# Query projections ahead of all convolutions in the selection block, with tap matrices built into the space of the normalised input

## The chip, the core and the metric

The kernel runs on one core of a Trainium2 chip. A core has a matrix engine (TensorE, PE in the profile), a vector engine (VectorE, DVE), a scalar engine (ScalarE, ACT), a general engine (GpSimd, POOL) and a queue that issues DMA transfers (SyncE, SP). Each runs its own list of instructions in order; they meet only at semaphores. The metric is the device time of one execution in microseconds (us).

## The reference

One layer of a decoder, over 1024 prompt positions and 8 x 8 sample positions (T = 1088 rows of D = 1024):

```python
h = rmsnorm(x, g_pre)
q, k, v, qi, ki, wi, ua, ub = split(h @ w_in)       # partial rotary on q, k, qi, ki
u = ua * sigmoid(ub)
score = sum_h wi_h * relu(qi_h . ki)                # keep the top 256 visible keys of each query
attn = softmax(q . k_selected) @ v_selected         # 8 heads, 2 key/value heads
c = causal depthwise conv(u, width 31) + b_dw; c = layernorm(c); c = c * sigmoid(c)
x = x + rmsnorm(concat(attn, c) @ w_out)
x = x + rmsnorm(relu(rmsnorm(x) @ w_up)^2 @ w_down)
```

## The kernel before

The kernel has four blocks, each closed by a barrier of all engines: projection and index scores, selection (`phase_select`), attention (`phase_attend`), output projection and MLP. The change lies in the selection block. Three things run in it side by side.

**The selection** (VectorE and ScalarE). A bit loop of 31 steps finds, for seven sets of rows, the bits of the 256th largest score: in each step VectorE counts over four sets (L1089), ScalarE over three (L945), and VectorE decides the bit from both. So a step ends when the later of the two is done. Two more counts follow, and then a tie loop over the seven sets: compare, running sum, select, add to the mask (L1164 to L1176). It needs the masks that ScalarE has scaled (`scale_masks`, L968).

**The convolution.** TensorE projects the 12 units of `u` (`uunits`, L1014) from the normalised input `hT`, ScalarE takes each unit from PSUM behind a step of the bit loop (`take_u`, L929 and L930; `behind` and `SIDE_PACE` say behind which), POOL multiplies (L838). After 12 units the rows go through DRAM into `up`, where each of the 32 groups (16 channels by 8 phases) holds one partition per channel and phase. A convolution of a group is then five matmul steps with a tap matrix of 128 x 640 values (`convolve`, L1051; the trace shows ten matmuls of 168 columns, two passes a step). POOL builds the tap matrix of a group by spreading the taps over a diagonal (`diagonal`, L853) into one of three slots in `stage`; group g waits until group g - 3 has been convolved. Three groups share a PSUM bank, ScalarE copies the bank back into `up` (`take_conv`, L936 and L938), and SP sends it to DRAM in two halves (L816): the first after 6 banks, the second after all 11.

**The queries.** `project_q` (L1040) computes 128 rows of q from `hT` into a bank, `take_q` (L919) copies them to one of three slots `zq`, POOL applies the rotary part (`rotate`, six small instructions, L868 to L875), TensorE turns them (`turn_q`, L1002), `take_turn` (L910) writes `qT`.

The order of TensorE is the list `EVENTS`: q0, c0, q1, c1, ..., q8, c8, c9, c10 (qi is a projection of a row block, ck a bank of convolutions), each over a bank of its own, six in turn. `turn_after` says after which event a query block is turned (two events later), and POOL follows the same list: rotate(i), then the three tap matrices of bank i. Since the tap matrices of a bank are queued behind the rotation of the same number, they wait for that projection and its copy.

At the end ScalarE copies the keys' high parts (`kH`, L983) and VectorE makes the low parts (L1182); then comes the barrier.

Of the kernel before, what the change touches and what calls it, by code (L numbers as in the profile page):

```python
# [26 lines left out]
P = 128  # L27
D = 1024
KC = D // P
# [3 lines left out]
T = SEQ + NB * NT  # L33
RT = SEQ // P + 1
# [53 lines left out]
MK_COLS = P * (SEQ // P) * (SEQ // P + 1) // 2  # L88

ACT_SETS = (2, 5, 6)  # L90
SIDE_PACE = 2.2

PH = 8
CG = P // PH
NCG = CC * PH
# [4 lines left out]
XRUN = XT - XS + 1  # L100
XO = T // PH
STEPS = 5
CONV_BANK = 3
# [530 lines left out]
def phase_select(nc, st, sem, sb_in, ps, bank, m, a, out):  # L634
# [15 lines left out]
    stage = sb_in(st, "stage", [P, 3 * STEPS * P])  # L650
    gate = stage[:, 0:768].rearrange("p (b t) -> p b t", b=2)
    ua = stage[:, 768:1536].rearrange("p (b t) -> p b t", b=2)
    wdiag = stage[:].rearrange("p (b n) -> p b n", b=3)
    dwp = sb_in(st, "dwp", [P, NCG, STEPS * PH])
    eye = sb_in(st, "eye", [P, CG])
    ulast = sb_in(st, "ulast", [P, CC, HIST])
# [66 lines left out]
    s_un = sem("s_un")  # L723


    EVENTS = [x for i in range(RT) for x in (("q", i), ("c", i))] + [("c", k) for k in range(RT, -(-NCG // CONV_BANK))]
    turn_after = {}
    for e, (kind, i) in enumerate(EVENTS):
        if kind == "q":
            turn_after.setdefault(min(max(e + 2, 4), len(EVENTS) - 1), []).append(i)  # L730
    TIE_ORDER = [NSET - 1] + list(reversed(range(NSET - 1)))

    def tie_sources(j):
# [27 lines left out]
    q_behind = {int(len(uunits) * SIDE_PACE + 1.4 * (i + 1)) + 1: i for i in range(3)}  # L761

    HIST_BIT = 4
    NCB = -(-NCG // CONV_BANK)

    conv_groups = lambda k: range(CONV_BANK * k, min(CONV_BANK * (k + 1), NCG))
    HEV = 2
# [1 line left out]
    with nc.Block() as block:  # L769
# [54 lines left out]
        @block.gpsimd  # L824
        def _(pool):
            nc.gpsimd.memset(usm[:], 0.0).then_inc(s_zero, 1)
            nc.gpsimd.memset(upr[:, :, :, 0:(HIST + 2) // PH], 0.0).then_inc(s_zero, 1)
            nc.gpsimd.memset(dwp[:], 0.0).then_inc(s_zero, 1)

            nc.gpsimd.tensor_copy(m["repb"][:], m["rep"][:])  # L830
            pool.wait_ge(s_c, 16 * CONSTS)
            for q, (n, c) in enumerate(uunits):
                t0, w = TCH[n]
                pool.wait_ge(s_g, q + 1)
                wp = min(w, SEQ - t0)
                x0 = (HIST + 2 + t0) // PH
                o = upr[:, c, :, x0:x0 + wp // PH].rearrange("p s x -> p x s")
                last = nc.gpsimd.tensor_tensor(o, ua[:, q % 2, 0:wp].rearrange("p (x s) -> p x s", s=PH),  # L838
                                               gate[:, q % 2, 0:wp].rearrange("p (x s) -> p x s", s=PH), ALU.mult)
                if wp < w:  # L840
                    nc.gpsimd.tensor_tensor(ulast[:, c, :], ua[:, q % 2, wp - HIST:wp], gate[:, q % 2, wp - HIST:wp],
                                            ALU.mult)
                    last = nc.gpsimd.tensor_tensor(unew[:, c, :], ua[:, q % 2, wp:w], gate[:, q % 2, wp:w], ALU.mult)
                last.then_inc(s_um, 1)
                if wp < w:
                    pool.wait_ge(s_um, q + 1)
                    nc.gpsimd.tensor_copy(usm[:, c, :, :].rearrange("p s (b x) -> p b s x", x=XS)[:, :, :, XS - 1],
                                          unew[:, c, :].rearrange("p (b t) -> p b t", t=NT)).then_inc(s_un, 1)

            def diagonal(g):  # L850
                if g >= 3:
                    pool.wait_ge(s_cg, g - 2)
                nc.gpsimd.tensor_tensor(wdiag[:, g % 3, :].rearrange("p (y c) -> p y c", c=CG),  # L853
                                        eye[:].unsqueeze(1).broadcast_to([P, STEPS * PH, CG]),
                                        dwp[:, g, :].unsqueeze(2).broadcast_to([P, STEPS * PH, CG]),
                                        ALU.mult).then_inc(s_dg, 1)

            def rotate(i):
                n = rows_of(i)
                zz = z[0:n, i % 3, :].rearrange("p (h d) -> p h d", d=HD)  # L860
                x1, x2 = zz[:, :, 0:HALF], zz[:, :, HALF:ROT]
                cos = cs[0:n, 0, i, :].unsqueeze(1).broadcast_to([n, NH, HALF])
                sin = cs[0:n, 1, i, :].unsqueeze(1).broadcast_to([n, NH, HALF])
                t = [rt[0:n, i % 2, k, :].rearrange("p (h d) -> p h d", d=HALF) for k in range(4)]
                pool.wait_ge(s_ze, i + 1)
                if i >= 2:
                    pool.wait_ge(s_rot, i - 1)
                nc.gpsimd.tensor_tensor(t[0], x1, cos, ALU.mult).then_inc(s_ro, 1)  # L868
                nc.gpsimd.tensor_tensor(t[1], x2, sin, ALU.mult).then_inc(s_ro, 1)
                nc.gpsimd.tensor_tensor(t[2], x2, cos, ALU.mult).then_inc(s_ro, 1)  # L870
                nc.gpsimd.tensor_tensor(t[3], x1, sin, ALU.mult).then_inc(s_ro, 1)
                pool.wait_ge(s_ro, 5 * i + 4)
                nc.gpsimd.tensor_tensor(x1, t[0], t[1], ALU.subtract).then_inc(s_ro, 1)
                pool.wait_ge(s_ro, 5 * i + 5)
                nc.gpsimd.tensor_tensor(x2, t[2], t[3], ALU.add).then_inc(s_rot, 1)  # L875

            pool.wait_ge(s_eye, 1)
            pool.wait_ge(s_dw, 16 * CC * PH)
            for g in conv_groups(0):
                diagonal(g)  # L880
            for kind, i in EVENTS:
                if kind == "q":
                    rotate(i)
                elif i >= 1:
                    for g in conv_groups(i):
                        diagonal(g)
            pool.wait_ge(s_dg, NCG)
            pool.wait_ge(s_z, RT)
            for kv in range(NKV):
                nc.gpsimd.memset(kL[(1 - kv) * HD:(2 - kv) * HD, kv, :].bitcast(F32), 0.0)  # L890

        @block.scalar
        def _(act):
# [74 lines left out]
                    nc.scalar.activation(mk, mk, ACT.Copy, scale=BIG, bias=-BIG).then_inc(s_ms, 1)  # L968

            taken = [i for it, i in q_behind.items() if it < BITS]  # L970
            for e, (kind, i) in enumerate(EVENTS):
                if kind == "c":
                    take_conv(i)
                elif i not in taken:
                    take_q(i)
                for q in turn_after.get(e, ()):
                    take_turn(q)
                if e == 4:
                    scale_masks()
            act.wait_ge(s_z, RT)  # L980
            for kv in range(NKV):
                for half in (kv, 1 - kv):
                    nc.scalar.copy(kH[half * HD:(half + 1) * HD, kv, :], kT[kv * HD:(kv + 1) * HD, 0:SEQ]).then_inc(s_kh, 1)  # L983

        @block.tensor
        def _(pe):
# [57 lines left out]
            def convolve(e, k):  # L1044
                bank_free(e)
                for g in conv_groups(k):
# [1 line left out]
                    pe.wait_ge(s_dg, g + 1)  # L1048
                    o = bank[2 + e % 6][:, (g % CONV_BANK) * XRUN:(g % CONV_BANK + 1) * XRUN]
                    for j in range(STEPS):  # L1050
                        last = nc.tensor.matmul(o, wdiag[:, g % 3, j * P:(j + 1) * P], up[:, g, j:j + XRUN],  # L1051
                                                start=(j == 0), stop=(j == STEPS - 1))
                    last.then_inc(s_cg, 1)

# [1 line left out]
            for e, (kind, i) in enumerate(EVENTS):  # L1056
                if kind == "q":
                    project_q(e, i)
                else:
                    convolve(e, i)  # L1060
                if e == 3:
                    turn_new_rows()
                if e == 4:
                    pe.wait_ge(s_te, HEV + 2)
                for q in turn_after.get(e, ()):
                    turn_q(q)
# [1259 lines left out]
```

## Time and profile before

| | us |
|---|---|
| median of 3 runs | 1841.5 (1841.31 to 1841.74) |
| profiled execution | 1840.0 |
| span in its trace | 1838.2 |
| PE busy in the span | 1600.2 (87%) |
| DVE, ACT, POOL busy | 671.6, 618.4, 408.8 |
| first u projection of the selection block | 252.4 |
| last of 12 units taken by ScalarE | 402.3 |
| end of the tie loop on VectorE | 479.2 |
| last convolution copied, second half of the DMAs issued | 573.7 |
| first instruction of attention | 581.6 |

Busy time is an average over blocks with different limits; TensorE is nearly full in the MLP and far from it in the selection block. Times in the timelines count from the start of the span, and the bracket behind an instruction is the idle time of its engine before it and what ended that. PEclk is the granted clock of TensorE as a share of 2.4 GHz.

### The profile page before, as it was taken

How to read it: one execution, taken by the hardware profiler on the slowest of the kernel's cores; microseconds unless marked ns; L12 is line 12 of the kernel's file. 1: busy time of each engine (PE TensorE's matmuls, PEld its weight loads, DVE VectorE, ACT ScalarE, POOL GpSimd, SP SyncE). 2: the span in 40 equal slices, each digit the busy share in tenths (PEclk: the TensorE clock that was granted, in tenths of full speed). 3: DMA queues.
4: the chain of work that ended last, by engine and by line, in shares of the span. 5: the costliest groups of instructions: out<-in, count | busy, mean ns of one | idle time of the engine just before them, and what ended most of it. 6: DMA issues, size and time to landing. Idle time of an engine off the chain costs nothing.

```text
span 1838.2 us, 22486 instructions
## 1 busy us (share of the span) xinstructions
PE 1600.2 (87%) x8760; PEld 1357.4 (74%) x8760; DVE 671.6 (37%) x1310; ACT 618.4 (34%) x1100; POOL 408.8 (22%) x434
## 2 busy tenths in 40 slices
PE   4798889955776998985984999999999999999996
PEld 2366446534455875664984999999999999999995
DVE  1236547779402543244007222222222222222225
ACT  2215539883103776244227312121121212021212
POOL 2232001025335121001227112221221222122112
PEclk9999989987888999987996999999999999999997
DMA  5011041312023101314110011111111111111102
GB/s 200 6 45 55 1 117 54 62 32 35 1 49 111 78 2 69 115 46 155 46 46 0 29 41 46 43 38 46 46 34 46 46 41 39 46 46 35 46 24 109
DMA packets 100053, 97.67 MB, mean 53 GB/s; under 512 B 14822, under 2 KB 88630, under 8 KB 97668
## 3 DMA queue, kind: packets, MB, share of 16 engines
q1 hardware_dynamic: 96492, 75.71, 14.5%
q0 software_dynamic: 3488, 20.98, 3.1%
q8 instruction: 47, 0.77, 0.2%
q14 instruction: 26, 0.21, 0.0%
HBM read 85.55 MB, written 11.45 MB: 53 GB/s over the span
## 4 chain that ended last, share of the span: by engine, by line
PE 47%; DVE 2%; ACT 2%; POOL 1%; DMA 1%; issue 0%; POOLq 0%; DVEq 0%; ACTq 0%
PE ps L2073 16%; PE ps L2075 16%; PE ps L2074 16%; DMA out_y_p<-y 1%; DVE xlo L2165 1%; POOL stat L1962 0%; ACT hrow L2027 0%; POOL x L1976 0%; DVE xlo L2163 0%; ACT y L2017 0%; DVE y L2225 0%; DVE y L2229 0%; POOL stat L1958 0%; DMA gpost<-in_g_mlp_post 0%; DVE hlo L2197 0%
## 5 line engine op out<-in xcount | busy, mean ns | idle before, releaser
L1951 POOL TENSOR_TENSOR wlo<-wraw,whi 128x1024 fp32r<-128x1024 f32 x72 | 173.9, 2416 | 723.2 <-ACT whi L1995 723.2
L2073 PE MATMUL ps<-xhi,whi 128*128 128x384 f32 (+1 forms) x960 | 314.7, 328 | 18.6 <-DVE xlo L2165 18.6
L2075 PE MATMUL ps<-xhi,wlo 128*128 128x384 f32 (+1 forms) x960 | 314.3, 327 | 0.0
L2074 PE MATMUL ps<-xlo,whi 128*128 128x384 f32 (+1 forms) x960 | 314.1, 327 | 0.0
L2073 PE MATMUL ps<-hhi,whi 128*128 128x384 f32 (+1 forms) x768 | 257.3, 335 | 16.8 <-DVE hlo L2197 16.8
L2074 PE MATMUL ps<-hlo,whi 128*128 128x384 f32 (+1 forms) x768 | 256.3, 334 | 0.0
L2075 PE MATMUL ps<-hhi,wlo 128*128 128x384 f32 (+1 forms) x768 | 256.2, 334 | 0.0
L2073 PEld LDWEIGHTS ps<-xhi,whi 128*128 128x128 f32 x960 | 181.3, 189 | 19.2 <-issue 18.2
L1995 ACT CAST whi<-wraw 128x1024 fp32r<-128x1024 f32 x72 | 75.5, 1049 | 345.9 <-PE ps L2075 345.8
L2216 DVE TENSOR_TENSOR moT<-ps,moT 128x384 f32<-128x384 f32 x168 | 90.1, 536 | 259.5 <-PE ps L2075 259.5
L2074 PEld LDWEIGHTS ps<-xlo,whi 128*128 128x128 f32 x960 | 181.3, 189 | 0.0
L2075 PEld LDWEIGHTS ps<-xhi,wlo 128*128 128x128 f32 x960 | 181.2, 189 | 0.0
L2073 PEld LDWEIGHTS ps<-hhi,whi 128*128 128x128 f32 x768 | 147.3, 192 | 18.8 <-DVE hlo L2197 14.0
L2204 DVE TENSOR_TENSOR rel<-rel 128x384 f32<-128x384 f32 (+1 forms) x96 | 51.5, 536 | 296.0 <-ACT rel L2050 296.0
L2074 PEld LDWEIGHTS ps<-hlo,whi 128*128 128x128 f32 x768 | 147.2, 192 | 0.0
L2075 PEld LDWEIGHTS ps<-hhi,wlo 128*128 128x128 f32 x768 | 147.2, 192 | 0.0
L2050 ACT ACTIVATE rel<-ps 128x384 f32<-128x384 f32 (+1 forms) x96 | 45.5, 474 | 276.7 <-PE ps L2075 276.7
L1014 PE MATMUL ps<-hT,w 128*128 128x384 f32 (+1 forms) x384 | 122.0, 481 | 13.5 <-DMA w<-in_w_u 8.6
L1014 PEld LDWEIGHTS ps<-hT,w 128*128 128x128 f32 x384 | 74.6, 195 | 59.9 <-issue 10.2
L1051 PE MATMUL ps<-up,stage 128*128 128x168 f32 x320 | 63.6, 371 | 59.1 <-POOL stage L853 59.1
L1089 DVE TENSOR_SCALAR_CACHE_REDUCE mask<-moT,cand 128x384 bf16<-128x384 f32 (+3 forms) x132 | 109.0, 882 | 1.1
L1051 PEld LDWEIGHTS ps<-up,stage 128*128 128x128 f32 x320 | 61.3, 242 | 62.2 <-issue 62.2
(268 smaller groups left out, 2238.0 us busy)
## 6 DMA issues: line engine op xcount, KB each, us to landing
wraw<-in_w_up SPq DMA_DIRECT2D x32, 512.0 KB, 4.1
wraw<-in_w_down SPq DMA_DIRECT2D x32, 512.0 KB, 3.4
x<-in_x SPq DMA_DIRECT2D x16, 512.0 KB, 7.4
w<-in_w_rows SPq DMA_DIRECT2D x2, 2048.0 KB, 10.3
w<-in_w_u SPq DMA_DIRECT2D x2, 2048.0 KB, 10.8
wraw<-in_w_out SPq DMA_DIRECT2D x8, 512.0 KB, 4.2
out_y_p<-y SPq DMA_DIRECT2D x8, 512.0 KB, 2.6
up<-by_channel SPq DMA_DIRECT2D x32, 86.0 KB, 4.1
```

Source lines behind the costliest of these rows:

```text
L1014: last = nc.tensor.matmul(bank[2 + 2 * (q % 3) + half][:, 0:w], wslot[c // 2][:, k, col:col + P], hT[:, k, t0:t0 + w], start=(k == 0), sto ...
L1051: last = nc.tensor.matmul(o, wdiag[:, g % 3, j * P:(j + 1) * P], up[:, g, j:j + XRUN], start=(j == 0), stop=(j == STEPS - 1))
L1089: last = nc.vector.tensor_scalar(mk, sc, against[0:n, j:j + 1].bitcast(F32), None, op, ALU.add, accum_out=count[0:n, j:j + 1])
L1951: nc.gpsimd.tensor_tensor(wlo[:, par, :], wraw[:, par, :], whi[:, par, :], ALU.subtract).then_inc(s_wlo, 1)
L1995: nc.scalar.copy(whi[:, j % 2, :], wraw[:, j % 2, :]).then_inc(s_whi, 1)
L2050: nc.scalar.activation(rel[:, b % 3, 0:TCH[c][1]], bank[b % NBK][:, 0:TCH[c][1]], ACT.Relu).then_inc(s_re, 1)
L2073: nc.tensor.matmul(o, wh, xh, start=first, stop=False)
L2074: nc.tensor.matmul(o, wh, xl, start=False, stop=False)
L2075: return nc.tensor.matmul(o, wl, xh, start=False, stop=last)
L2165: nc.vector.tensor_tensor(in_time(xlo, t0, w), by_phase(t0, w), in_time(xhi, t0, w), ALU.subtract).then_inc(s_mlo, 1)
L2204: nc.vector.tensor_tensor(rel[:, b % 3, 0:w], rel[:, b % 3, 0:w], rel[:, b % 3, 0:w], ALU.mult).then_inc(s_sq, 1)
L2216: nc.vector.tensor_tensor(dst, src, dst, ALU.add).then_inc(s_ad, 1)
```

## The change

The projections of all nine query blocks now stand ahead of all eleven banks of convolutions on TensorE. The first three tap matrices stay in `stage`; the others go into 13 slots laid over `hT`, which nothing reads after the last projection, so `diagonal(3)` waits for all nine projections (`s_z`), and from group 16 on a slot waits for the group 13 before it. POOL's order is now: tap matrices 0 to 2, rotations 0 to 6, tap matrices 3 to 7, rotation 7, tap matrices 8 to 10, rotation 8, tap matrices 11 to 31. ScalarE turns and takes in an order of its own, copies the key parts after bank 2, and takes the other banks last. `SIDE_PACE` goes from 2.2 to 2.08, which moves the takes of u from steps 3, 5, 7, 9, 12, 14, 16, 18, 20, 23, 25, 27 of the bit loop to 3, 5, 7, 9, 11, 13, 15, 17, 19, 21, 23, 25, and the takes of q0 and q1 from steps 28 and 30 to 27 and 28, with q2 behind step 30.

```diff
-SIDE_PACE = 2.2
+SIDE_PACE = 2.08
...
-    wdiag = stage[:].rearrange("p (b n) -> p b n", b=3)
+    WN = STEPS * P
+    WS = 3
+    WH = KC * T // WN
+    flat = hT[:].rearrange("p k t -> p (k t)")
+    wdiag = [stage[:, g * WN:(g + 1) * WN] if g < WS else flat[:, (g - WS) % WH * WN:((g - WS) % WH + 1) * WN]
+             for g in range(NCG)]
...
-    EVENTS = [x for i in range(RT) for x in (("q", i), ("c", i))] + [("c", k) for k in range(RT, -(-NCG // CONV_BANK))]
-    turn_after = {}
-    for e, (kind, i) in enumerate(EVENTS):
-        if kind == "q":
-            turn_after.setdefault(min(max(e + 2, 4), len(EVENTS) - 1), []).append(i)
+    NCB = -(-NCG // CONV_BANK)
+    EVENTS = [("q", i) for i in range(RT)] + [("c", k) for k in range(NCB)]
+    turn_after = {6: (0, 1), 7: (2,), 8: (3, 4), 9: (5,), 10: (6,), 11: (7,), 12: (8,)}
...
             def diagonal(g):
-                if g >= 3:
-                    pool.wait_ge(s_cg, g - 2)
-                nc.gpsimd.tensor_tensor(wdiag[:, g % 3, :].rearrange("p (y c) -> p y c", c=CG),
+                if g == WS:
+                    pool.wait_ge(s_z, RT)
+                if g >= WS + WH:
+                    pool.wait_ge(s_cg, g - WH + 1)
+                nc.gpsimd.tensor_tensor(wdiag[g].rearrange("p (y c) -> p y c", c=CG),
...
-            for g in conv_groups(0):
+            for g in range(WS):
                 diagonal(g)
-            for kind, i in EVENTS:
-                if kind == "q":
-                    rotate(i)
-                elif i >= 1:
-                    for g in conv_groups(i):
-                        diagonal(g)
+            for i in range(RT - 2):
+                rotate(i)
+            for g in range(WS, WS + 5):
+                diagonal(g)
+            rotate(RT - 2)
+            for g in range(WS + 5, WS + 8):
+                diagonal(g)
+            rotate(RT - 1)
+            for g in range(WS + 8, NCG):
+                diagonal(g)
...
-            for e, (kind, i) in enumerate(EVENTS):
-                if kind == "c":
-                    take_conv(i)
-                elif i not in taken:
-                    take_q(i)
-                for q in turn_after.get(e, ()):
-                    take_turn(q)
-                if e == 4:
+            for i in range(RT - 3):
+                if i == 0:
+                    for q in range(len(taken), 3):
+                        take_q(q)
+                take_turn(i)
+                take_q(i + 3)
+                if i == 1:
                     scale_masks()
-            act.wait_ge(s_z, RT)
+            for i in range(RT - 3, RT):
+                take_turn(i)
+                take_conv(i - RT + 3)
             for kv in range(NKV):
                 for half in (kv, 1 - kv):
                     nc.scalar.copy(kH[half * HD:(half + 1) * HD, kv, :], kT[kv * HD:(kv + 1) * HD, 0:SEQ]).then_inc(s_kh, 1)
+            for k in range(3, NCB):
+                take_conv(k)
...
-                if e == 3:
+                if e == 1:
                     turn_new_rows()
-                if e == 4:
+                if e == 6:
                     pe.wait_ge(s_te, HEV + 2)
```

On TensorE, from the last projection of u on (`w,hT` is a query projection, `up,stage` or `up,hT` a bank of convolutions, `identf,zq` a turn of query blocks, four instructions each, `ulast` and `unew` the turn of the new convolution rows), before:

```order
L1040 MATMUL ps<-w,hT 128x512 x8
L1051 MATMUL ps<-up,stage 128x168 x15
L1040 MATMUL ps<-w,hT 128x512 x8
L1051 MATMUL ps<-up,stage 128x168 x15
L1023 MATMUL ps<-identf,ulast 30x128 x4
L1026 MATMUL ps<-identf,unew 64x128 x4
L1040 MATMUL ps<-w,hT 128x512 x8
L1002 MATMUL ps<-identf,zq 128x128 x8
L1051 MATMUL ps<-up,stage 128x168 x15
```

and now:

```order
L1051 MATMUL ps<-w,hT 128x512 x16
L1034 MATMUL ps<-identf,ulast 30x128 x4
L1037 MATMUL ps<-identf,unew 64x128 x4
L1051 MATMUL ps<-w,hT 128x512 x40
L1013 MATMUL ps<-identf,zq 128x128 x8
L1051 MATMUL ps<-w,hT 128x512 x8
L1013 MATMUL ps<-identf,zq 128x128 x4
L1051 MATMUL ps<-w,hT 64x512 x8
L1013 MATMUL ps<-identf,zq 128x128 x8
L1062 MATMUL ps<-up,stage 128x168 x15
L1013 MATMUL ps<-identf,zq 128x128 x4
L1062 MATMUL ps<-up,hT 128x168 x15
```

All 9 x 8 projections come first, with the wait for ScalarE's copies of the new rows behind the seventh; the first bank stands behind the turn of query block 4.

On POOL, around the rotation of query block 7 (`zq` and `rtq` are the rotation, `eye,dwp` a tap matrix), before:

```order
L873 TENSOR_TENSOR zq<-rtq 128x8x8
L875 TENSOR_TENSOR zq<-rtq 128x8x8
L853 TENSOR_TENSOR stage<-eye,dwp 128x640 x3
L868 TENSOR_TENSOR rtq<-zq,csq 128x64
L869 TENSOR_TENSOR rtq<-zq,csq 128x64
L870 TENSOR_TENSOR rtq<-zq,csq 128x64
L871 TENSOR_TENSOR rtq<-zq,csq 128x64
L873 TENSOR_TENSOR zq<-rtq 128x8x8
L875 TENSOR_TENSOR zq<-rtq 128x8x8
L853 TENSOR_TENSOR stage<-eye,dwp 128x640 x3
```

and now:

```order
L877 TENSOR_TENSOR zq<-rtq 128x8x8
L879 TENSOR_TENSOR zq<-rtq 128x8x8
L857 TENSOR_TENSOR hT<-eye,dwp 128x640 x5
L872 TENSOR_TENSOR rtq<-zq,csq 128x64
L873 TENSOR_TENSOR rtq<-zq,csq 128x64
L874 TENSOR_TENSOR rtq<-zq,csq 128x64
L875 TENSOR_TENSOR rtq<-zq,csq 128x64
L877 TENSOR_TENSOR zq<-rtq 128x8x8
L879 TENSOR_TENSOR zq<-rtq 128x8x8
L857 TENSOR_TENSOR hT<-eye,dwp 128x640 x3
```

Before, three tap matrices stood between two rotations, in the slots of `stage`; now five and three, in slots over `hT`, and only six tap matrices still have a rotation right in front of them.

## Rows read from the trace of the kernel before

**Rows 1.** The page, chain that ended last: shares of the span by engine.
```profile
PE 47%; DVE 2%; ACT 2%; POOL 1%; DMA 1%; issue 0%; POOLq 0%; DVEq 0%; ACTq 0%
```

**Rows 2.** Busy time by engine in two stretches of 20 us (columns in the first line).
```profile
core 0: us, PE busy (x) PEld busy (x) DVE busy (x) ACT busy (x) POOL busy (x), PEclk, DMA share, GB/s
440.00:460.00 20.00, 7.12 (x32) 6.79 (x33) 19.76 (x11) 4.90 (x9) 17.00 (x9) 0.57 0.00 1
500.00:520.00 20.00, 16.42 (x59) 10.66 (x58) 0.00 (x0) 1.64 (x4) 5.47 (x9) 0.91 0.17 31
```

**Rows 3.** Waits, 400 to 600 us: engine, line, waited for: us in total, times, longest.
```profile
POOL rtq L868 <- ACT zq L919: 88.2, 8, 12.2
...
PE ps L1051 <- POOL stage L853: 59.1, 9, 15.4
```

**Rows 4.** Timeline, PE: start us, us, engine, line, operation, count, [idle before it].
```profile
383.49 7.11 PE L1040 MATMUL ps<-w,hT 128*128 128x512 f32 x16 [3.51 <-ACT stage L930]
...
507.93 6.19 PE L1051 MATMUL ps<-up,stage 128*128 128x168 f32 x30 [3.58 <-POOL stage L853]
513.96 7.03 PE L1040 MATMUL ps<-w,hT 128*128 128x512 f32 x16
520.83 0.60 PE L1002 MATMUL ps<-identf,zq 128*128 128x128 f32 x4
```

**Rows 5.** Timeline, POOL, where VectorE runs counts or nothing.
```profile
404.62 3.73 POOL L853 TENSOR_TENSOR stage<-eye,dwp 128x640 f32<-128x640 f32 x3
...
521.69 0.32 POOL L868 TENSOR_TENSOR rtq<-zq,csq 128x64 f32<-128x64 f32 x1 [11.45 <-ACT zq L919]
...
523.31 0.32 POOL L875 TENSOR_TENSOR zq<-rtq 128x64 f32<-128x64 f32 x1
...
565.55 1.27 POOL L853 TENSOR_TENSOR stage<-eye,dwp 128x640 f32<-128x640 f32 x1 [0.15 <-PE ps L1051]
...
568.40 1.27 POOL L853 TENSOR_TENSOR stage<-eye,dwp 128x640 f32<-128x640 f32 x1 [0.15 <-PE ps L1051]
```

**Rows 6.** Timeline, POOL, beside VectorE's tie loop.
```profile
437.58 4.39 POOL L868 TENSOR_TENSOR rtq<-zq,csq 128x64 f32<-128x64 f32 x1 [12.25 <-ACT zq L919]
...
451.47 5.69 POOL L853 TENSOR_TENSOR stage<-eye,dwp 128x640 f32<-128x640 f32 x3
466.99 1.50 POOL L868 TENSOR_TENSOR rtq<-zq,csq 128x64 f32<-128x64 f32 x1 [9.83 <-ACT zq L919]
...
472.09 4.62 POOL L853 TENSOR_TENSOR stage<-eye,dwp 128x640 f32<-128x640 f32 x3
```

**Rows 7.** Timeline, DVE, the tie loop: two early instructions and the last.
```profile
437.43 4.43 DVE L1168 TENSOR_TENSOR_SCAN w<-w 64x2056 f32<-64x2056 bf16 x1
441.89 2.51 DVE L1171 SCALAR_TENSOR_TENSOR w<-w,need 64x2056 bf16<-64x2056 f32 x1
...
478.61 0.56 DVE L1176 SCALAR_TENSOR_TENSOR mask<-w,mask 128x384 bf16<-128x384 bf16 x1
```

**Rows 8.** Timeline, ACT, at the end of the bit loop.
```profile
398.37 0.83 ACT L945 ACTIVATE mask<-moT,cand 128x640 bf16<-128x640 f32 x1 [0.91 <-DVE cand L1106]
...
402.32 0.42 ACT L929 ACTIVATE stage<-ps 128x320 f32<-128x320 f32 x1
...
407.27 0.56 ACT L919 COPY zq<-ps 128x512 f32<-128x512 f32 x1
```

**Rows 9.** Timeline, the DMA queue of SP (issues), both halves of the outgoing convolution.
```profile
514.75 7.49 SPq L816 DMA_DIRECT2D by_time<-up  x16
523.96 0.34 SPq L820 DMA_DIRECT2D moT<-by_time  x1
573.69 7.47 SPq L816 DMA_DIRECT2D by_time<-up  x16
```

**Rows 10.** Windows of 1 us in one bank of convolutions (columns as in rows 2).
```profile
493.00:494.00 1.00, 1.00 (x5) 1.00 (x5) 0.00 (x0) 0.00 (x0) 0.17 (x1) 0.50 0.00 0
495.00:496.00 1.00, 1.00 (x9) 1.00 (x8) 0.00 (x0) 0.00 (x0) 0.00 (x0) 1.00 0.00 0
```

More of the change, by code:

```diff
@@ L763, in phase_select @@
     HIST_BIT = 4
-    NCB = -(-NCG // CONV_BANK)
     conv_groups = lambda k: range(CONV_BANK * k, min(CONV_BANK * (k + 1), NCG))
@@ L1050, in convolve @@
                     for j in range(STEPS):
-                        last = nc.tensor.matmul(o, wdiag[:, g % 3, j * P:(j + 1) * P], up[:, g, j:j + XRUN],
+                        last = nc.tensor.matmul(o, wdiag[g][:, j * P:(j + 1) * P], up[:, g, j:j + XRUN],
                                                 start=(j == 0), stop=(j == STEPS - 1))
```

## The prediction

> **What bounds the kernel now.** I read the chain that ended last first. Its parts name TensorE for 47% of the span and hardly anything else [rows 1], all of it the late MLP, so it says nothing of the block that changes; but the MLP and attention follow behind barriers, so what the selection block gives is what the kernel gives. Next come busy times over short stretches of that block: from 500 to 520 us TensorE is busy for 16.4 of 20 us, VectorE for none, ScalarE for 1.6 and POOL for 5.5; from 440 to 460 us TensorE has 7.1 while VectorE is full and POOL at 17.0 [rows 2]. So the first part runs beside VectorE, and the second is a chain through TensorE with holes. The waits name them: TensorE waits 59.1 us in 9 waits for tap matrices, and POOL 88.2 us in 8 waits for copies of a projection [rows 3]. POOL has time, but it stands in the wrong place of its list. The timeline shows one round: bank of convolutions 6.2 us, projection 6.9, turn 0.6, idle 3.58 for POOL, 17.1 in all [rows 4]. In that idle time POOL does a rotation of 1.9 us (521.69 to 523.63) and the first tap matrix, 1.24 of 3.73 [rows 5]. The block ends when the last bank is copied: SP then issues 16 transfers in 7.47 us from 573.69 on [rows 9], and attention starts.
>
> **The bit loop.** A step takes 4.95 us (402.32 to 407.27), and ScalarE idles 0.91 us in a step without a take [rows 8]; a take of q costs 0.56, so one more of them there costs nothing as long as its projection is ready. By the step length, u9, u10 and u11 are taken at 402.3 - 6 x 4.95 = 372.6, 382.5 and 392.4 us, ten us earlier than now. q0 and q1 need u9's banks, and run from 373.5 to 387.5 (about 7 each). The turn of the new rows then waits until POOL has multiplied u11: 2.3 us behind its take (402.32 to 404.62, [rows 5, 8]), so at 394.7. Five more projections of 6.87 (the distance 513.96 to 520.83, [rows 4]), 1 us for the turn and some 2 at the low clock bring TensorE to 432; turns 0 and 1 to 433; q7, turn 2 and q8 to 447.5. q0, q1 and q2 are taken at 402, 407 and 417, so TensorE has 15 us or more in hand at each. The wait for ScalarE's copies of the new rows is over at 420 and costs nothing behind q6. Seven of nine projections are now hidden under the bit loop and the two counts behind it, where only two or three were. SIDE_PACE alone gives nothing; it opens the banks.
>
> **POOL beside the tie loop.** This is where the price of the change lies. Rotation 3 can start at 434, when the tie loop starts. Without VectorE six rotation instructions take 1.9 us [rows 5]; beside it the first instruction alone took 4.39, and the rotation with three tap matrices took from 437.58 to 457.16, 19.6 us for 5.7 us of work [rows 6]. The first instruction ends at 441.97, within 0.1 us of the end of the running sum at 441.86 [rows 7]: POOL is held until VectorE's instruction is done. Further on, where VectorE's instructions are short, the same work took 466.99 to 476.71, 9.7 us: a rate of 0.59. The two tap triples beside it give 3.73/5.69 = 0.66 and 3.73/4.62 = 0.81.
>
> Rotations 3 and 4 cost from 434 to about 453.5. Then I take the rate 0.6. Rotations 5 and 6 (3.8 us) go to 460; tap matrices 3 to 7 (6.2) to 470; rotation 7, tap matrices 8 to 10 and rotation 8 (7.5) to 483. Tap matrix 11 is there at 484. VectorE, now disturbed by more POOL work, ends its loop about 5 us later than 479.2, near the same time; nothing waits for it but the low key parts, 2.4 us and long before the end. Bounds for tap matrix 11: at rate 1 from 453.5 on, 473; at the first stretch's rate of 5.7/19.6 = 0.29 until 484 and 1 behind it, 493.
>
> The Trainium skill, SBUF — State Buffer, section "Who interferes with whom", says that a VectorE instruction with two inputs in SBUF and a POOL instruction that reads SBUF exclude each other for a whole instruction, in order of issue. The trace agrees for the running sum. By that rule alone each of eight tap matrices would wait for a VectorE instruction of about 1.4 us, 2.6 in place of my 2.1, and tap matrix 11 would come 4 us later, the kernel at 1787; my sum goes by the measured rates.
>
> **The convolutions.** At full clock TensorE convolves a group in 1.43 us: POOL's tap matrices from 565.55 to 568.40 wait for one group each, (568.40 - 565.55) / 2 apart [rows 5]. At half clock it is twice that, 2.8 us (5 matmuls in a window of 1 us at a granted clock of 0.50 against 9 at 1.00, both counts with cut ends, [rows 10]). A tap matrix costs POOL 1.24 us free of waiting, so once VectorE is out of the way POOL keeps ahead of TensorE, and TensorE is the bound. Bank 0 runs at 454 to 460 behind the turn of block 4. Groups 3 to 10 follow their tap matrices, about 2 us apart, slower than 1.43; turns 5 to 8 (0.6 each) lie in the gaps, except 8. From 484: 21 groups by 1.43 = 30.0, the turn 0.6, the last copy 0.6, and 0.8 for a start at the low clock: 516.
>
> **The tail.** SP's first half must be through before the second: bank 5 (groups 15 to 17) is taken at about 494, behind the key copies; issue 7.49 and landing end 9.2 later (514.75 to 523.96, [rows 9]), at 503, before 516. So the second half starts at once. Key copies and low parts, which lay behind the last bank, are hidden now as before: SP's 7.47 us covered them. The clearing of the key halves by POOL, 2 us, is over with the last tap matrix. Attention starts earlier by the whole difference.
>
> Sum: 573.7 - 516 = 57.7 us. Against the profiled execution, 1840.0 us (span 1838.2 and 1.8 around it): 1782.3. The median of the runs is 1.5 us above that execution, so I say 1783. As a check, what TensorE still has before it when the tie loop begins: before, six projections (41), 26 groups by 6.19/3 = 2.06 (54), turns (4) and by difference some 37 of waiting for POOL, to 573; now two projections (14), 32 groups (47), turns (5) and 18 of waiting, to 516. The gain is four projections done earlier, 19 us of waiting, and 7 us of clock, since the groups run in one piece.
>
> **The rivals.**
>
> 1. *POOL gets through earlier.* If tap matrix 11 comes at 473, TensorE is the bound from bank 1 on: 460 + 29 x 1.43 + 2.4 for turns + 0.6 = 504.5, a saving of 69 and 1772. For it: 0.81 in the second triple [rows 6]. Against it: rotations do far worse than tap matrices, and two of them stand in front.
> 2. *TensorE at the low clock, or POOL held longer.* Waiting for tap matrices 2 us apart, it might lose its clock, and the later groups go at 2.8 us. Rows show 0.50 at the start of a bank, after 3.6 us of idling, and 1.00 within 4 us of steady work [rows 4, 10]. If the clock is low for half of 29 groups, 14 x 1.4 = 20 us are added; or tap matrix 11 comes at 493, 9 us. 1792 to 1803; I give the clock and the longer hold 0.08 each. Against it: at 2.8 us a group TensorE is never idle with matrices 2 us apart, and steady work brought the clock back each time. [...]
> 3. *Slower than before.* The takes of q0, q1 and q2 now stand in the bit loop in ScalarE's fixed order, and VectorE waits for ScalarE in each step. A projection that is late by n us there stops the selection for n us, and all that follows. TensorE is 15 us ahead at q2, the closest, and the change has 57 us to lose, so it must be 72 us late there, as if every projection took twice its 6.87 us and the units of u did too. 1845 if so. Nothing in the trace points to it.
> 4. *It does not do what it says*: the projections stay behind something that ends with the bit loop, such as the wait for the new rows at 420. Then all nine end only at 420 + 9 x 6.87 = 482, tap matrix 3 cannot start before (it needs all nine), and 29 groups take to 482 + 41.5 + 3 = 527: 1794. Against it: only q7 and q8 lie behind that wait in the list.
>
> **How the numbers follow.** The forecast has 0.60 (1776 to 1790), rival 1 0.14, rival 2 0.16, rival 4 0.06, rival 3 0.03, and 0.01 for a result near the old time. The range 1768 to 1799 leaves out rival 3, the end of rival 2, and what is below rival 1. A measurement of this kernel tells 0.2%, 3.7 us, from no change; all cases but the last two lie far outside it: faster 0.96, same 0.01, slower 0.03.
>
> **What would show it.** In the profile after, six projections would start before 425, all nine be done by 450; the 9 waits of convolutions for tap matrices be gone but for bank 1 to 3 (some 15 to 25 us together); tap matrices 3 to 10 lie at 460 to 483 at 1.5 to 2.2 us each; the last 20 groups run without a gap at 1.43 us, clock 1.0; SP's second half begins at 516. The bit loop must still end at 418 to 419. I would be wrong if ScalarE idles in it before a take of q, if tap matrices 3 to 10 take more than 3 us each, or if attention or the MLP change their length.

## The result, and the profile after

The changed kernel takes 1782.3 us (median of 4 runs, 1781.0 to 1783.0) against 1841.6 (1841.3 to 1842.3) in the same comparison: 0.968 of the time, 95% interval 0.966 to 0.969. The forecast was 1783. The profiled execution took 1781.0 us with a span of 1779.2.

The beginning of the bit loop differs by up to 4.3 us between the traces (260.76 to 265.09 us), and what differs lies ahead of the block. So I measure the block from its first count by ScalarE to the second half of the outgoing convolution on SP. These two rows are the first counts, of before and of after:

```profile
262.80 0.83 ACT L945 ACTIVATE mask<-moT,cand 128x640 bf16<-128x640 f32 x1 [19.30 <-DVE cand L1106]
```
```profile
260.98 0.83 ACT L953 ACTIVATE mask<-moT,cand 128x640 bf16<-128x640 f32 x1 [19.20 <-DVE cand L1117]
```

And the timeline of SP's queue after, which answers to [rows 9]:

```profile
494.43 7.47 SPq L818 DMA_DIRECT2D by_time<-up  x16
...
514.27 7.44 SPq L818 DMA_DIRECT2D by_time<-up  x16
```

Before, 573.69 - 262.80 = 310.9 us; after, 514.27 - 260.98 = 253.3. The block is 57.6 us shorter (the sum said 57.7). The spans differ by 59.0; the rest is the start, which lies 1.8 us earlier in this trace, less 0.4 behind the block. I call this distance the block's length below; each length is read from one trace. In all traces here TensorE's first instruction of attention follows 10.0 to 10.1 us behind SP's second half (583.74 before, 524.29 after), so what shortens the block shortens the kernel.

TensorE's timeline after, against [rows 4]:

```profile
371.75 13.97 PE L1051 MATMUL ps<-w,hT 128*128 128x512 f32 x32 [0.22 <-ACT stage L938]
392.68 1.03 PE L1034 MATMUL ps<-identf,ulast 128*30 128x128 f32 x4 [6.95 <-POOL unew L845]
...
394.36 35.85 PE L1051 MATMUL ps<-w,hT 128*128 128x512 f32 x80
...
450.80 6.56 PE L1062 MATMUL ps<-up,stage 128*128 128x168 f32 x30
...
463.87 6.91 PE L1062 MATMUL ps<-up,hT 128*128 128x168 f32 x30 [6.08 <-POOL hT L857]
...
476.79 1.66 PE L1062 MATMUL ps<-up,hT 128*128 128x168 f32 x10 [2.72 <-POOL hT L857]
...
483.00 1.67 PE L1062 MATMUL ps<-up,hT 128*128 128x168 f32 x10 [1.25 <-POOL hT L857]
...
484.98 28.79 PE L1062 MATMUL ps<-up,hT 128*128 128x168 f32 x200
```

There are three stretches: projections q0 to q6 under the bit loop and the two counts behind it, with one hole of 7 us; then banks with four waits, one for a rotation (3.9 us) and three for tap matrices; and the last 20 groups without a gap, 28.79 / 20 = 1.44 us each. The waits from 380 to 530 us, where [rows 3] had 59.1 us in 9 waits of TensorE and 88.2 in 8 of POOL:

```profile
POOL rtq L872 <- ACT zq L927: 29.3, 4, 13.1
...
PE ps L1062 <- POOL hT L857: 10.1, 3, 6.1
...
PE ps L1034 <- POOL unew L845: 7.0, 1, 7.0
...
PE ps L1013 <- POOL zq L879: 3.9, 1, 3.9
```

Windows of the same stretch (columns as in [rows 2]):

```profile
440.00:460.00 20.00, 13.88 (x55) 9.58 (x53) 19.65 (x15) 3.21 (x6) 19.69 (x17) 0.83 0.00 0
...
464.00:468.00 4.00, 4.00 (x15) 4.00 (x16) 3.93 (x3) 0.00 (x0) 4.00 (x3) 0.50 0.00 0
468.00:472.00 4.00, 4.00 (x28) 4.00 (x27) 3.97 (x3) 0.75 (x2) 4.00 (x3) 0.91 0.00 0
...
484.00:512.00 28.00, 28.00 (x198) 27.75 (x197) 22.90 (x2) 8.59 (x21) 25.37 (x22) 1.00 0.34 81
```

From 440 to 460 us TensorE had 7.1 of 20 before and has 13.9 now; VectorE and POOL are both full there. POOL's timeline, against [rows 5] and [rows 6]:

```profile
435.59 4.53 POOL L879 TENSOR_TENSOR zq<-rtq 128x64 f32<-128x64 f32 x1
...
462.21 8.96 POOL L857 TENSOR_TENSOR hT<-eye,dwp 128x640 f32<-128x640 f32 x5
...
475.38 4.36 POOL L857 TENSOR_TENSOR hT<-eye,dwp 128x640 f32<-128x640 f32 x3
...
481.59 25.89 POOL L857 TENSOR_TENSOR hT<-eye,dwp 128x640 f32<-128x640 f32 x21
```

POOL builds its tap matrices in three runs behind a rotation, of 5, 3 and 21. A tap matrix costs 1.79 us (8.96 / 5) and 1.45 (4.36 / 3) beside the tie loop, 1.23 (25.89 / 21) behind it. VectorE's timeline, against [rows 7], has a row that nobody forecast:

```profile
435.57 4.43 DVE L1179 TENSOR_TENSOR_SCAN w<-w 64x2056 f32<-64x2056 bf16 x1
...
477.09 1.51 DVE L1187 SCALAR_TENSOR_TENSOR mask<-w,mask 128x384 bf16<-128x384 bf16 x1
486.88 22.91 DVE L1193 TENSOR_TENSOR keys<-kT,keys 64x1024 fp32r<-64x1024 f32 x2 [8.28 <-ACT keys L992]
```

The two low parts of the keys take 22.9 us together, from 486.88 to 509.79, while POOL builds its 21 tap matrices. They are done 4.5 us before SP's second half begins at 514.27, so nothing waits for them.

### The profile page after: what moved, and what is told of

It reads as the page before. It is cut to its first block, busy times and chain, and to the rows that moved or that the text cites. A ratio compares the mean times of both kernels' runs of the same rounds, so it can differ in the third digit from the quotient of the medians.

```text
span 1779.2 us, 22486 instructions
## 1 busy us (share of the span) xinstructions
PE 1584.5 (89%) x8760; PEld 1344.1 (76%) x8760; DVE 693.8 (39%) x1310; ACT 618.1 (35%) x1100; POOL 419.2 (24%) x434
## 4 chain that ended last, share of the span: by engine, by line
PE 49%; DVE 2%; ACT 2%; POOL 1%; DMA 1%; issue 0%; POOLq 0%; DVEq 0%; ACTq 0%
PE ps L2084 16%; PE ps L2086 16%; PE ps L2085 16%; DMA out_y_p<-y 1%; DVE xlo L2176 1%; POOL stat L1973 0%; ACT hrow L2038 0%; POOL x L1987 0%; DVE xlo L2174 0%; ACT y L2028 0%; DVE y L2236 0%; DVE y L2240 0%; POOL stat L1969 0%; DMA gpost<-in_g_mlp_post 0%; DVE hlo L2208 0%
## 5 line engine op out<-in xcount | busy, mean ns | idle before, releaser
L2084 PEld LDWEIGHTS ps<-xhi,whi 128*128 128x128 f32 x960 | 181.4, 189 | 19.1 <-issue 18.2
L465 PE MATMUL ps<-w,hT 128*128 128x328 f32 (+3 forms) x256 | 95.4, 527 | 0.0
L465 PEld LDWEIGHTS ps<-w,hT 128*128 128x128 f32 (+1 forms) x256 | 47.4, 190 | 39.3 <-issue 27.6
```

The lines of the kernel that those rows point to most:

```text
L465: last = nc.tensor.matmul(bank[2 + u % 2][0:n, 0:w], hT[:, k, i * P:i * P + n], wslot[g % 2][:, k, 0:w], start=(k == 0), stop=(k == KC - 1))
L2084: nc.tensor.matmul(o, wh, xh, start=first, stop=False)
```

## Where the gain comes from

The forecast gave the credit to the projections done early and called SIDE_PACE a mere opener. The first five experiments take the parts apart. Ratios are to the kernel before in the same comparison, with 95% intervals. That kernel's median was between 1837 and 1842 us, so across sections ratios are compared, or the block's lengths, and not times.

**SIDE_PACE alone, in the kernel before.**

```
-SIDE_PACE = 2.2
+SIDE_PACE = 2.08
```

> The kernel before with SIDE_PACE 2.08 alone. The prediction says that this alone gives nothing: 1841.6 us. Rival, from the row of the rotation beside the tie loop: with q1 and q2 taken ten us earlier, rotation 2 runs at about 426 us, ahead of the tie loop, and takes 2 us in place of 14; the fourth bank of convolutions starts at about 457 in place of 473.5, and some 12 us remain at the end: 1829.

1827.6 us, 0.993 (0.992 to 0.994): the rival's value. The block's length is 560.99 - 263.61 = 297.4, 13.5 less. The first bank of convolutions starts 9.9 us earlier, counted from the start of the block (396.94 - 263.61 against 406.04 - 262.80), and in POOL's timeline the third rotation is now through before the tie loop starts:

```profile
396.94 5.97 PE L1051 MATMUL ps<-up,stage 128*128 128x168 f32 x30 [15.44 <-POOL stage L853]
```
```profile
428.32 0.32 POOL L868 TENSOR_TENSOR rtq<-zq,csq 128x64 f32<-128x64 f32 x1 [12.21 <-ACT zq L919]
...
430.23 3.73 POOL L853 TENSOR_TENSOR stage<-eye,dwp 128x640 f32<-128x640 f32 x3
```

In [rows 6] the same rotation and three tap matrices took 19.6 us. The waits of this kernel from 400 to 600 us:

```profile
PE ps L1051 <- POOL stage L853: 37.3, 9, 11.7
```

[Rows 3] has 59.1 us in the same stretch, but with the first bank's wait of 15.4, which here ends before 400. Without it that is 43.7 against 37.3. So most of the 13.5 us is that the chain starts 9.9 us earlier and keeps that lead through the tie loop; the waits give the smaller part. The sentence "SIDE_PACE alone gives nothing" is wrong in the old order.

**POOL's list alone.** The kernel before, with the tap matrices of bank i put ahead of rotation i; the order on TensorE and ScalarE, the three buffers of `stage` and the pace of 2.2 stay. A tap matrix needs nothing of a projection.

```
-            for kind, i in EVENTS:
-                if kind == "q":
-                    rotate(i)
-                elif i >= 1:
+            for i in range(NCB):
+                if i >= 1:
...
+                if i < RT:
+                    rotate(i)
```

> The kernel before with POOL's list alone changed (tap matrices of a bank ahead of the rotation of the same number), SIDE_PACE left at 2.2. Theory (the tie loop holds POOL whatever came ten us earlier, so the two edits overlap): 1786, some 2 us above the same with 2.08. Rival (the two add up, 13 us for the pace by the run that changed it alone): 1797.

1782.3 us, 0.970 (0.969 to 0.972), the block's length 514.82 - 260.76 = 254.1 against the changed kernel's 253.3. One reordered list gives, within what can be told here, the whole gain, with the projections where they were. TensorE's waits for tap matrices from 400 to 600 us, against 59.1 in [rows 3]:

```profile
PE ps L1051 <- POOL stage L853: 17.0, 5, 15.4
```

The longest, 15.4, is that of the first bank, at the end of the bit loop. Behind it 1.6 us are left in four waits.

**The same list with the pace of 2.08.**

> The kernel before, order of TensorE and ScalarE as it was, SIDE_PACE 2.08, and only POOL's list changed: the tap matrices of a bank stand before the rotation of the same number, in the three slots of stage. Theory (order on POOL is the whole effect; all projections first is not needed): no 3.6 us of idling and no half clock in a round, 11.9 us a round in place of 17.1, the last bank at about 517: 1785. Rival (projections must be out of the way): the rounds keep most of their length, 1810 or more.

1783.6 us, 0.969 (0.968 to 0.970): the theory's value. TensorE's timeline shows a round, against [rows 4]:

```profile
481.74 4.44 PE L1051 MATMUL ps<-up,stage 128*128 128x168 f32 x30
486.02 7.03 PE L1040 MATMUL ps<-w,hT 128*128 128x512 f32 x16
492.88 0.60 PE L1002 MATMUL ps<-identf,zq 128*128 128x128 f32 x4
```

A round is 493.32 - 481.74 = 11.6 us where it was 17.1. Of the 5.5 us, 3.6 are the idle time and 1.75 the bank's start at the low clock (6.19 to 4.44); both go because the three tap matrices are built while TensorE projects. The interval overlaps that at 2.2: pace and list do not add. With 2.08 TensorE comes to the turn of a query block while POOL still does that rotation beside the tie loop; it waits 8.17 us there, which it does not at 2.2, and the bank behind it takes 6.80 us:

```profile
454.83 1.11 PE L1002 MATMUL ps<-identf,zq 128*128 128x128 f32 x4 [8.17 <-POOL zq L875]
```

So what the pace wins ahead of the tie loop is lost in it.

**No space in `hT`.** The changed kernel with all 32 tap matrices in the three buffers of `stage`.

```
-    wdiag = [stage[:, g * WN:(g + 1) * WN] if g < WS else flat[:, (g - WS) % WH * WN:((g - WS) % WH + 1) * WN]
+    wdiag = [stage[:, g % WS * WN:(g % WS + 1) * WN]
...
-                if g == WS:
-                    pool.wait_ge(s_z, RT)
-                if g >= WS + WH:
-                    pool.wait_ge(s_cg, g - WH + 1)
+                if g >= WS:
+                    pool.wait_ge(s_cg, g - WS + 1)
```

> The changed kernel with all tap matrices in the three slots of stage, group g waiting for the convolution of group g - 3; nothing is laid over the normalised input. Theory (order decides, and with three slots TensorE still sets the pace at 1.43 us a group): 1782 to 1784. Rival (the space is what lets POOL run ahead, and without it POOL and TensorE wait for each other): at least 0.3 us a group over 29 groups, 1791 or more. By the theory VectorE's low key parts also get in between two tap matrices again, 1.2 us each in place of 22.9 for both.

1783.8 us, 0.970 (0.968 to 0.971), length 253.1. The space in the normalised input is worth nothing that can be told here: POOL needs 1.24 us for a tap matrix and TensorE 1.43 for a group, so three buffers feed it. POOL and VectorE in that kernel:

```profile
490.21 1.27 POOL L855 TENSOR_TENSOR stage<-eye,dwp 128x640 f32<-128x640 f32 x1 [0.21 <-PE ps L1060]
```
```profile
490.34 4.45 DVE L1191 TENSOR_TENSOR keys<-kT,keys 64x1024 fp32r<-64x1024 f32 x2 [8.28 <-ACT keys L990]
```

Where POOL waits 0.15 to 0.2 us for each buffer, the low parts of the keys take 4.45 us, not 22.9.

**The old pace in the changed kernel.**

> The changed kernel with SIDE_PACE back at 2.2. Theory (POOL beside the tie loop sets the start of the convolutions): rotation 3 starts at 440 in place of 432, tap matrix 3 at about 468 in place of 462, so 1788 against 1782. Rival (the chain of projections on TensorE sets it): all ten us of delay come out at the end, 1792. Rival (POOL is held by the tie loop whatever its start): 1782.

1783.6 us, 0.970 (0.968 to 0.972), length 517.45 - 261.73 = 255.7, 2.4 more than with 2.08: near the rival by which the loop holds POOL whatever its start. POOL starts rotation 3 at 442.82 where it was 431.83, but does rotations 3 and 4 in 10.0 us (to 452.79) where it took 18.0 (to 449.80), and reaches tap matrix 3 only 3 us later than in the changed kernel:

```profile
465.21 8.96 POOL L857 TENSOR_TENSOR hT<-eye,dwp 128x640 f32<-128x640 f32 x5
```

What POOL does ahead of time meets the long instructions at the front of VectorE's loop, and most of the lead is lost there.

## What holds the rest

**Without the tie loop.** This kernel leaves VectorE's tie loop out, so ties are not added to the masks.

```
-            for q, j in enumerate(TIE_ORDER):
...
-                last.then_inc(s_tadd, 1)
```

> The changed kernel without VectorE's tie loop (keys equal to the threshold are left out of the masks). Theory (what is left of waiting before bank 4 is POOL held by the tie loop): rotations 3 to 6 take 2 us each, tap matrix 3 follows the ninth projection, banks run from 446 without gaps to about 496: 1764. Rival (turns and ScalarE's order hold TensorE, not POOL): at most 5 us less, 1777 or more.

1762.0 us, 0.959 (0.957 to 0.960), length 496.37 - 262.15 = 234.2, 19.1 us less: the theory's value. Its POOL row and its PE rows:

```profile
450.04 6.19 POOL L857 TENSOR_TENSOR hT<-eye,dwp 128x640 f32<-128x640 f32 x5
```
```profile
447.22 4.44 PE L1062 MATMUL ps<-up,stage 128*128 128x168 f32 x30
...
467.07 28.79 PE L1062 MATMUL ps<-up,hT 128*128 128x168 f32 x200
```

A tap matrix is back at 1.24 us, bank 0 at full clock. So what POOL and VectorE do to one another is worth 19 us here: 13.3 of waiting (14.0 less the 0.6 that is left), 4.6 of clock (6.56 and 6.91 against 4.44 for banks 0 and 1), and about 1 in the turns and starts.

**New rows turned later.** The hole of 6.95 us at 392.68 is TensorE's list: the turn stands before q2.

```
-                if i == 1:
+                if i == 2:
                     scale_masks()
...
-                if e == 1:
+                if e == 3:
                     turn_new_rows()
```

> The changed kernel with the turn of the new convolution rows behind q3 in place of q1 (TensorE idles 7 us before it now), and the masks scaled behind the take of q5 in place of q4. Theory (what costs is POOL work that falls into the tie loop): q8 ends at 437 in place of 445, rotations 3 to 5 run before the tie loop at 2 us each, tap matrix 11 comes at about 474 in place of 483: 1773. Rival (the tie loop holds POOL until it ends whatever was done ahead, as going back to 2.2 changed next to nothing): 1781 or more.

1779.3 us, 0.966 (0.965 to 0.968), length 249.5: 3.8 us shorter, not the 9 of the theory. By their ratios the two kernels cannot be told apart. Bank 0 starts 13.8 us earlier, counted from the start of the block (440.51 - 264.52 against 450.80 - 260.98). But behind it TensorE waits 19.1 us for tap matrices in four waits (8.96, 0.75, 6.50 and 2.92), where it waited 10.1 in three:

```profile
440.51 4.44 PE L1062 MATMUL ps<-up,stage 128*128 128x168 f32 x30
...
454.36 6.37 PE L1062 MATMUL ps<-up,hT 128*128 128x168 f32 x30 [8.96 <-POOL hT L857]
...
471.49 3.14 PE L1062 MATMUL ps<-up,hT 128*128 128x168 f32 x10 [6.50 <-POOL hT L857]
```
```profile
452.94 10.25 POOL L857 TENSOR_TENSOR hT<-eye,dwp 128x640 f32<-128x640 f32 x5
```

The time won moves POOL's work into the front of the tie loop, where VectorE's instructions are long: a tap matrix costs 2.05 us there.

**Two more buffers,** so that five tap matrices are ready before the tie loop, on top of the last experiment (`WS = 5`: a spare tensor, and space left in the second slot of the weights).

> As the run with the rows later, and two more slots for tap matrices that are free before the tie loop (five ahead of the bit loop's end in place of three), with POOL's list: rotations 0 to 5, taps 5 and 6, rotation 6, taps 7 to 9, rotation 7, taps 10 to 12, rotation 8, the rest. Theory: bank 1 needs one tap matrix from the tie loop in place of three; tap matrices run about 5 us further ahead: 1768. Rival (TensorE now waits for the rotations of blocks 6 to 8, not for taps): the same as the run with the rows later, within 2 us.

1779.0 us, 0.966 (0.964 to 0.967), the rival's value; length 510.64 - 262.83 = 247.8. TensorE then waits for a rotation instead:

```profile
455.58 1.11 PE L1019 MATMUL ps<-identf,zq 128*128 128x128 f32 x4 [7.59 <-POOL zq L882]
```

**Keys copied last** (ScalarE copies banks 3 to 10 first), to see whether the 22.9 us of the low parts cost anything.

```
+            for k in range(3, NCB):
+                take_conv(k)
...
-            for k in range(3, NCB):
-                take_conv(k)
```

> The changed kernel with ScalarE's copies of the high key parts behind the last bank, as they were before. Theory (they and VectorE's low parts lie beside the 16 transfers of SP, 7.5 us, in either place): 1782, and the two low parts take 1.2 us each in place of 22.9 for both. Rival (they reach past the transfers): 2 to 4 us more.

1783.5 us, 0.969 (0.968 to 0.971), length 515.04 - 262.24 = 252.8: the same time. Behind POOL's run a low part takes 1.22 us:

```profile
515.99 1.22 DVE L1193 TENSOR_TENSOR keys<-kT,keys 64x1024 fp32r<-64x1024 f32 x1 [36.61 <-ACT keys L994]
```

**Gaps in POOL's run.** The same changed kernel with one wait more: from tap matrix 11 on POOL may be three groups ahead of TensorE at most.

```
-                if g >= WS + WH:
-                    pool.wait_ge(s_cg, g - WH + 1)
+                if g >= WS + 8:
+                    pool.wait_ge(s_cg, g - 2)
```

> The changed kernel, with one more wait only: from tap matrix 11 on POOL may be at most three groups ahead of TensorE (it still writes to its own place in the normalised input). POOL's run of 21 tap matrices, 25.9 us without a gap, then gets gaps of some 0.15 to 0.2 us after every 1.24 us, since TensorE takes 1.43 a group. Theory: what kept VectorE out of its first low part of the keys (21.7 us) is that POOL's instructions follow each other without a gap; with gaps each of the two low parts takes 2 to 2.5 us, as with three buffers in stage (4.45 for two). Rival: the place of the tap matrices or the way the keys fall in time did it, and the first low part still takes 15 us or more. Both expect the same total, 1781 to 1786 us, since nothing near the end waits for the low parts.

1781.7 us beside 1841.4 in one run each, length 515.89 - 262.62 = 253.3. The two low parts take 4.45 us: the gaps let VectorE in. VectorE's and POOL's rows:

```profile
488.04 4.45 DVE L1193 TENSOR_TENSOR keys<-kT,keys 64x1024 fp32r<-64x1024 f32 x2 [8.28 <-ACT keys L992]
```
```profile
501.21 1.27 POOL L857 TENSOR_TENSOR hT<-eye,dwp 128x640 f32<-128x640 f32 x1 [0.15 <-PE ps L1062]
```

**Tap matrices on VectorE.** In the changed kernel, VectorE builds tap matrices 3 to 15 behind the first set of ties, and POOL only rotates and then builds 16 to 31, at most five groups ahead of TensorE. The turns of blocks 5 to 8 and ScalarE's copies of them stand one or two banks later; the cut shows VectorE's part alone.

```
+                if q == 0:
+                    dve.wait_ge(s_z, RT)
+                    for g in range(WS, WS + NV):
+                        nc.vector.tensor_tensor(wdiag[g]..., ALU.mult).then_inc(s_dv, 1)
```

> The changed kernel with tap matrices 3 to 15 built by VectorE behind the first set of the tie loop (and the ninth projection), POOL doing only rotations there and tap matrices 16 to 31 later, each at most five groups ahead; turns of blocks 5 to 8 stand one to two banks later. Theory (POOL shut out by the tie loop is what TensorE still waits for, and it goes away if VectorE does that work itself, at some 0.75 us each by the 1.22 us of a 64x1024 product): bank 1 follows bank 0 at about 457, the last bank ends at about 502: 1770. Rival (the loop and POOL's rotations, later by 10 us, hold the turns and so the banks): 1780 or more.

1777.7 us, 0.967 (0.966 to 0.968), no difference from the changed kernel's 0.968 that can be told, and not the theory's 1770; length 510.71 - 260.86 = 249.9. VectorE is quick, 0.74 us each, but its 13 instructions in a row hold one of POOL's for 9.80 us, and bank 0 stands in TensorE's list behind the turn of that rotation:

```profile
446.24 9.63 DVE L1201 TENSOR_TENSOR hT<-eye,dwp 128x640 f32<-128x640 f32 x13
```
```profile
446.25 9.80 POOL L876 TENSOR_TENSOR rtq<-zq,csq 128x64 f32<-128x64 f32 x1
```
```profile
459.09 1.12 PE L1017 MATMUL ps<-identf,zq 128*128 128x128 f32 x4 [13.27 <-POOL zq L880]
```

**Both: tap matrices on VectorE, new rows turned later.** Now rotation 4 is through before the tie loop, and bank 0 does not wait for it.

> As the run with VectorE's tap matrices, and the new rows turned behind q3, masks scaled behind q5. Theory: q8 ends 7 us earlier, bank 0 starts at 440, rotations 3 to 5 lie ahead of the tie loop, but tap matrices still follow its first set at 447: 3 to 6 us less, 1766. Rival (as with POOL's taps, the loop decides): the same within 2 us.

1764.3 us, 0.960 (0.959 to 0.961), 0.8% below the changed kernel, and the intervals do not meet: the fastest complete kernel here. Its length, 501.15 - 264.37 = 236.8, is 2.6 us over that of the one without a tie loop. Its rows on PE, VectorE and POOL:

```profile
440.40 4.44 PE L1069 MATMUL ps<-up,stage 128*128 128x168 f32 x30
450.68 6.65 PE L1069 MATMUL ps<-up,hT 128*128 128x168 f32 x30 [5.83 <-DVE hT L1201]
```
```profile
449.73 9.63 DVE L1201 TENSOR_TENSOR hT<-eye,dwp 128x640 f32<-128x640 f32 x13
...
473.82 12.03 DVE L1195 SCALAR_TENSOR_TENSOR mask<-usm,mask 128x768 bf16<-128x768 bf16 x1
```
```profile
449.86 9.68 POOL L878 TENSOR_TENSOR zq<-rtq 128x64 f32<-128x64 f32 x1
```

POOL is held as long as before (9.68 us), but nothing that comes soon needs it. Alone, each of the two gives at most 4 us of length; together 16.5 (253.3 to 236.8). With the turn alone TensorE waits 19.1 us for tap matrices, with VectorE's tap matrices alone 13.3 us for a rotation; together it waits 5.83 and 2.42.

## Why the prediction was right, step by step

- **What bounds the block.** Right: a wait in POOL's list, not its work. POOL waits 29.3 us for copies of a projection, not 88.2, and the reordered list alone takes the wait away.
- **The bit loop.** q0 and q1 run from 371.75 to 385.7 (forecast 373.5 to 387.5), ScalarE takes q0, q1 and q2 (401.23, 406.19, 416.11) without idling before them, and the loop is as long as before, 155.9 us from the first count to the last bit against 156.1. The turn of the new rows ends its wait at 392.68 (forecast 394.7), the last projection at 445.3 (447.5).
- **POOL beside the tie loop.** Tap matrix 3 starts at 462.2 (forecast 460), 1.79 us each (2.1 assumed), tap matrix 11 at 482.8 (484). The rate of 0.6 is a little low: 1.24 / 1.79 = 0.69. VectorE's loop ends at 478.6, not at 484, and so the third run goes at full rate.
- **TensorE's waits** in the convolutions are 10.1 + 3.9 = 14.0 us, 18 assumed. The last 20 groups run at 1.44 us. Banks 0 and 1 lose 2.1 and 2.5 us to the low clock (forecast: 0.8 at one start). Waits 4 us shorter and clock 4 us dearer cancel: that part of the agreement is luck.
- **The check of the sum** had 19 us of waits and 7 of clock. From the tie loop on, the trace before has waits of 15.12, 6.78, four times 3.58 and 3.40, 39.6 in all, so the waits give 25.6 us. Its 26 groups took 51.4 us there, and the 32 groups now take 51.6, so the groups give nothing, not 7: six more of them are left at that time, which uses up what the clock gives.
- **The step that failed** is "SIDE_PACE alone gives nothing; it opens the banks", and with it the sum's credit to four projections done early. The pace alone gives 13.5 us of length in the old order and 2.4 in the new. POOL's list alone gives 56.8 of the block's 57.6 us (310.9 to 254.1), with the projections late. The sum was right because it counted what TensorE still had before it and how long it would wait; its split into causes only adds up times that belong together, and does not test which edit earns them. In the old order a late projection fills the time in which POOL builds tap matrices, which is as good as having it done.
- **Rivals.** 1 (POOL earlier) fell: tap matrix 11 came at 483. 2 (the clock, or POOL held to 493) fell here: the granted clock is 0.50 at the start of bank 0, behind a wait of 3.9 us, and again from 464 to 468 us, behind one of 6.1; then it is 0.91 and 1.00, through waits of 2.7 and 1.3 us. The Trainium skill, TensorE: Matmul & The Clock Gate, section "HAM oscillation — how this bites in real kernels", describes waits between groups of matmuls behind each of which the clock is low again. The trace agrees for the two longer waits and shows nothing of it behind the two shorter ones. No threshold follows from this: with the new rows turned later the granted clock is 1.00 from 481 to 482 us and 0.51 in the next microsecond, behind a wait of 2.92 us that began 7 us after the end of the one of 6.50. 3 fell: the bit loop did not wait. 4 fell: seven projections were done by 430.2.
- **The signs.** Tap matrices 3 to 10 lie at 462 to 480 us at 1.79 and 1.45 us each, and SP's second half begins at 514.3 (516). The waits for tap matrices are 10.1 us, less than the 15 to 25 expected. What follows the block keeps its length: 1264.9 us from SP's second half to the end of the span, 1264.5 before.
- **Not forecast:** the 22.9 us of the low key parts. The sum had them hidden, and they were, 12 us ahead of attention (509.8 against 522).

## What to carry to other kernels

Where an engine's list holds an instruction that needs nothing behind one that waits for its neighbour, exchange the two before anything larger is rebuilt: here the tap matrices put ahead of the rotations gave what a new order of nine projections and buffers in the normalised input gave. A sum of times (work left plus waits) can forecast a total well and still say nothing of which edit earns it; only one edit alone does. Where two engines exclude each other, the fastest kernel here gave the work to the quicker one (0.74 against 1.24 us a tap matrix) and let nobody wait for the other in that stretch; the first without the second gave next to nothing.

## What the runs showed that I had not expected

- **A run of queued instructions keeps the other engine out from first to last.** One VectorE instruction that takes 1.22 us free took 21.7 us (22.91 less 1.22 for the second) beside POOL's run of 21 tap matrices; with the new rows turned later a TENSOR_SCALAR was held from 479.56 on, beside this run of POOL:

```profile
479.56 26.32 DVE L1175 TENSOR_SCALAR w<-moT,v_bits 128x384 bf16<-128x384 f32 x1
```
```profile
479.78 25.88 POOL L857 TENSOR_TENSOR hT<-eye,dwp 128x640 f32<-128x640 f32 x21
```

  It goes the other way as well: 13 instructions of VectorE in a row held one of POOL's for 9.8 us. The Trainium skill, SBUF — State Buffer, section "Who interferes with whom", says that the first to issue has the pair of SBUF ports that VectorE and POOL share for the whole instruction. The trace agrees, but shows more: between back-to-back instructions the waiting engine did not get in. With gaps of 0.15 to 0.2 us between POOL's it did, with one wait more and no other edit (4.45 us for the two low parts, 22.9 without gaps; one run). In the fastest kernel a mask instruction of VectorE took 12.03 us beside the first half of POOL's run of 16 tap matrices, and nothing waited for it. Such a hold is free only while there is time in hand: with the new rows turned later the tie loop ended at 508.1 in place of 478.6 and the low parts at 510.5, 3.5 us before SP's second half.
